# Loading four modulation chunks ahead of the tokens in the prologue of a fused two-block transformer kernel

## What is computed

```
silu_c, silu_cc = silu(c), silu(c_ctx)
mod_lat = silu_c  @ ada_w[0] + ada_b[0]      # 6 x 1024: sh1, sc1, ga1, sh2, sc2, ga2
mod_ctx = silu_cc @ ada_w[0] + ada_b[0]
u_lat = rms_norm(h_lat, g_mix[0]) * (1 + sc1) + sh1
u_ctx = rms_norm(h_ctx, g_mix[0]) * (1 + csc1) + csh1
q, k, v = split(u_lat @ na_wqkv[0]), and the same for u_ctx
```

## Time and profile before

| what | value |
|---|---|
| time, median of 3 runs | 2734.12 us |
| lowest and highest of them | 2729.07 and 2738.08 us |
| the profiled execution's own time | 2735.49 us |
| its span, first to last instruction | 2733.7 us |
| mean granted clock of TensorE | 0.992 |
| TensorE busy | 2619.9 us, 96% of the span |
| VectorE busy | 1549.0 us, 57% |
| ScalarE busy | 1072.7 us, 39% |
| GpSimd busy | 875.9 us, 32% |
| sixteen DMA engines | 26.3% of their span |

### The profile page before, as it was taken

The page is one execution under the profiler, slowest core; times in us unless marked ns, Lnnn a source line. Parts: engine busy times, 40 slices in busy tenths (PEclk is TensorE's granted clock), DMA queues, the critical chain, the costliest instruction groups (busy, mean ns, idle before and its releaser), DMA issues. The chain is left out here.

```text
span 2733.7 us, 38265 instructions
## 1 busy us (share of the span) xinstructions
PE 2619.9 (96%) x14748; PEld 2129.2 (78%) x14748; DVE 1549.0 (57%) x2903; ACT 1072.7 (39%) x1864; POOL 875.9 (32%) x651
## 2 busy tenths in 40 slices
PE   6899999999999999999899999999999999999997
PEld 4787786788888888766668888787778888788886
DVE  5434444687777778555664444544556445516555
ACT  4444544422222223565542322354553434542222
POOL 1211121243333333021124444333334333444443
PEclk9999999999999999999999999999999999999999
DMA  6323333223333332110012222322213221222221
GB/s 246 114 86 96 113 101 101 85 104 106 106 105 106 106 107 72 52 47 32 32 47 95 105 92 92 96 64 76 77 48 102 69 86 62 94 93 93 93 93 62
DMA packets 69652, 243.02 MB, mean 89 GB/s; under 512 B 11780, under 2 KB 29700, under 8 KB 49288
## 3 DMA queue, kind: packets, MB, share of 16 engines
q1 hardware_dynamic: 69512, 241.15, 26.3%
HBM read 239.02 MB, written 2.10 MB: 88 GB/s over the span
## 5 line engine op out<-in xcount | busy, mean ns | idle before, releaser
L248 POOL TENSOR_TENSOR w_lo<-w_raw,w_hi 128x512 fp32r<-128x512 f32 x612 | 820.8, 1373 | 1737.3 <-ACT w_hi L241 604.9
L287 PE MATMUL bank<-u_hi,w_hi 128*128 128x512 f32 (+1 forms) x1952 | 732.3, 375 | 10.8 <-DVE u_lo L548 5.0
L289 PE MATMUL bank<-u_hi,w_lo 128*128 128x512 f32 (+1 forms) x1952 | 719.6, 369 | 0.0
L288 PE MATMUL bank<-u_lo,w_hi 128*128 128x512 f32 (+1 forms) x1952 | 718.7, 368 | 0.0
L287 PEld LDWEIGHTS bank<-u_hi,w_hi 128*128 128x128 f32 x1952 | 368.6, 189 | 82.0 <-issue 10.7
L288 PEld LDWEIGHTS bank<-u_lo,w_hi 128*128 128x128 f32 x1952 | 368.8, 189 | 62.1 <-issue 2.5
L289 PEld LDWEIGHTS bank<-u_hi,w_lo 128*128 128x128 f32 x1952 | 368.4, 189 | 62.5
L1088 DVE SCALAR_TENSOR_TENSOR resid<-bank,mod,resid 128x512 f32<-128x512 f32 (+1 forms) x384 | 242.1, 658 | 141.2 <-PE bank L289 136.4
L287 PE MATMUL bank<-hid_hi,w_hi 128*128 128x512 f32 (+1 forms) x768 | 275.5, 359 | 0.0
L289 PE MATMUL bank<-hid_hi,w_lo 128*128 128x512 f32 (+1 forms) x768 | 273.0, 355 | 0.0
L288 PE MATMUL bank<-hid_lo,w_hi 128*128 128x512 f32 (+1 forms) x768 | 272.1, 354 | 0.0
(11 more groups left out here) (411 smaller groups left out, 3885.3 us busy)
## 6 DMA issues: line engine op xcount, KB each, us to landing
w_raw<-stream SPq DMA_DIRECT2D x150, 1024.0 KB, 4.9
w_raw<-stream SPq DMA_DIRECT2D x56, 512.0 KB, 4.5
ada_ring<-stream SPq DMA_DIRECT2D x48, 512.0 KB, 4.7
bias<-bias SPq DMA_DIRECT2D x192, 64.0 KB, 2.3
ada_more<-stream SPq DMA_DIRECT2D x6, 1024.0 KB, 12.4
resid<-h SPq DMA_DIRECT2D x2, 1536.0 KB, 9.2
w_raw<-stream SPq DMA_DIRECT2D x8, 256.0 KB, 3.9
out<-resid SPq DMA_DIRECT2D x8, 256.0 KB, 2.0
```

The costliest lines, as they stand in the source:

```text
L248: ins = eng.tensor_tensor(m.wl[:, s, w], m.raw[:, s, w], m.wh[:, s, w].bitcast(F32), ALU.subtract)
L287: pe.matmul(out, lh, rh, start=start, stop=False)
L288: pe.matmul(out, lh, rl, start=False, stop=False)
L289: return pe.matmul(out, ll, rh, start=False, stop=stop)
```

## The change

SyncE issues modulation chunks 0 to 3 first, then the lower tokens, the weight chunk and the upper tokens; chunks 4 to 7 stand behind them as before. TensorE and VectorE do rows, copies, columns and gains of pairs 0 and 1 ahead of the norm's adds and sum. The rows of chunks 4 and 5 stand behind the norm's sum, ahead of projections 0 and 1; columns 2 and the rows of chunks 6 and 7 stand between projections 1 and 2, columns 3 between projections 3 and 4. On VectorE the copy of row 4 stands ahead of round 0, that of row 5 ahead of round 1; pair 2's columns and the copies of rows 6 and 7 ahead of round 2, pair 3's columns ahead of round 3. On ScalarE the high part of the weights moves from behind the eighth square to behind the fourth. In `na_stage` SyncE waits for the low part of the first weight chunk before it loads the next one into the same slot, which the wait for chunk 4's row implied before.

```diff
@@ Norm.act
             if k == KT // 2:
+                between()
                 act.wait_ge(second, 16)
             act.activation(self.sq[:, k % 2, :], m.h[:, k, 0:tok], ACT.Square).then_inc(*A.mark(f"n_sq{k}"))
-        between()
@@ prologue, vector
+                for p in range(2):
+                    copy(2 * p)
+                    copy(2 * p + 1)
+                    modulated(p)
                 norm.dve(dve)
...
+                def beside(p):
                     if p == 0:
+                        copy(4)
+                        own(dve, D)
                         dve.wait_ge(A.sem, A.at("n_rs"))
-                latent.dve(dve, 2, modulated)
+                    if p == 1:
+                        copy(5)
+                    if p == 2:
+                        modulated(2)
+                        copy(6)
+                        copy(7)
+                        own(dve, D)
+                    if p == 3:
+                        modulated(3)
+                        own(dve, D)
+                latent.dve(dve, 2, beside)
@@ prologue, tensor
-                rows(0)
-                rows(1)
-                norm.pe(pe)
+                for p in range(2):
+                    rows(2 * p)
+                    rows(2 * p + 1)
+                    columns(p)
                 pe.matmul(m.bank[:, 5, 0:2], cst(m, "ones"), m.misc[:, 2:4], start=True,
                           stop=True).then_inc(*E.mark("lamdot"))
-                columns(0)
+                norm.pe(pe)
+                rows(4)
+                rows(5)
                 pe.wait_ge(m.G.sem, m.G.at("w0_lo"))
-                for p in range(FIRST // 2):
-                    if 2 * p + 2 < FIRST:
-                        rows(2 * p + 2)
-                        rows(2 * p + 3)
-                    first_projection(2 * p)
-                    if 2 * p + 2 < FIRST:
-                        columns(p + 1)
-                    first_projection(2 * p + 1)
+                first_projection(0)
+                first_projection(1)
+                columns(2)
+                rows(6)
+                rows(7)
+                first_projection(2)
+                first_projection(3)
+                columns(3)
+                for k in range(4, KT):
+                    first_projection(k)
@@ na_stage, sync
                 load_bias(0, 2, bias_last_in)
+                sp.wait_ge(*m.first_low)
                 for n in range(2, 5):
                     load(fills[n])
```

More of the change, by code:

```diff
@@ L617, in prologue @@
                        only=0)
[L618 to L623, removed]
+        A.plan(["exp_c"] + Norm.act_steps[:KT // 2] + ["w0_hi"] + Norm.act_steps[KT // 2:] + ["exp_lam"])
+        pairs = [(f"row{2 * p}", f"row{2 * p + 1}", f"mod{p}", f"gsc{p}") for p in range(FIRST // 2)]
+        D.plan(["eps", "zero", "sig1", "sig2", "silu", "sel", *pairs[0], *pairs[1]] + Norm.dve_steps +
+               ["q1", "q2", "q3", *pairs[2], *pairs[3], "lam1", "lam2"])
+        E.plan(["ada0", "ada1", "columns0", "ada2", "ada3", "columns1", "lamdot", "n_sum", "ada4", "ada5", "columns2",
+                "ada6", "ada7", "columns3"])
         m.G.plan(["w0_lo"])
         m.ring_read = E.sem, E.at("ada4")
+        m.first_low = m.G.sem, m.G.at("w0_lo")
         for block in (m.block,):
@@ L631, in _, with chunk @@
                 sp.dma_start(m.cst[:, :], m.in_cst[:, 0:CST["swap"][1]]).then_inc(m.small_in, 16)
[L632 to L635, removed]
+                def chunk(n):
                     if n >= 4:
@@ L638, in _ @@
                         sp.wait_ge(landed[n % 4], 16 * (n // 4))
-                    sp.dma_start(slots[n % 4], m.stream[c]).then_inc(landed[n % 4], 16)
+                    sp.dma_start(slots[n % 4], m.stream[ORDER[n]]).then_inc(landed[n % 4], 16)
+                for n in range(4):
+                    chunk(n)
+                sp.dma_start(m.h[:, 0:KT // 2, :], m.in_h[:, 0:KT // 2, :]).then_inc(h_in, 16)
+                sp.dma_start(m.raw[:, 0, :], m.stream[N_ADA]).then_inc(m.first_in, 16)
+                sp.dma_start(m.h[:, KT // 2:KT, :], m.in_h[:, KT // 2:KT, :]).then_inc(rest_in, 16)
+                for n in range(4, FIRST):
+                    chunk(n)
             @block.scalar
@@ L681, in _, with copy, modulated @@
                                   ALU.add).then_inc(*D.mark("sel"))
+                def copy(n):
+                    dve.wait_ge(E.sem, E.at(f"ada{n}"))
+                    if n >= 2:
+                        dve.wait_ge(E.sem, E.at(f"columns{n // 2 - 1}"))
+                    dve.tensor_copy(part[:, n % 2, :], m.bank[:, 2 + n % 2, 0:2 * P]).then_inc(*D.mark(f"row{n}"))
+                def modulated(p):
+                    dve.wait_ge(E.sem, E.at(f"columns{p}"))
+                    mod_add(dve, m, pmod[:, 4 * p:4 * p + 4], p)
+                    mod_add(dve, m, pmod[:, 16 + 4 * p:20 + 4 * p], 4 + p).then_inc(*D.mark(f"mod{p}"))
+                    own(dve, D)
+                    mod_gain(dve, m, 4 + p).then_inc(*D.mark(f"gsc{p}"))
+                for p in range(2):
+                    copy(2 * p)
+                    copy(2 * p + 1)
+                    modulated(p)
                 norm.dve(dve)
```

## The result

The changed kernel takes **2737.0 us** (median of 13 runs, 2734.71 to 2743.15), the kernel before 2733.3 (13 runs, 2728.89 to 2738.08). Paired, the ratio is **1.0019, interval 1.0011 to 1.0027**: slower by 5.2 us, 3.0 to 7.4. That is no change by the 0.3% named ahead, and yet it can be told from zero. The forecast was 2736.6 and +2.5 us. (The two medians lie 3.7 us apart; the 5.2 is the paired ratio less 1, times 2733.)

A forecast was written before the change was run, and what follows sets the result against it. Bound: when the prologue hands on the first projection. First scaling 8.8 us later less 7.1 of gaps gives +1.7 (+1.2 to +4.6 by TensorE's clock); +2.5 chosen on the median 2734.12, so 2736.6 us, range 2729.5 to 2743.

The forecast's parts named there:

- the hand-over: Start of ScalarE's squares of the first projection, 54.11 before; forecast at 55 to 58.5 us.
- Landings: Prologue loads: lower tokens land at 19.2 instead of 9.28, behind 4 MiB more at 2.49 us per MiB.
- The adds: Norm on VectorE: one square of 0.84 and four adds of 1.05 left; sums ready at 30.6, before 19.05.
- From the sums to the first scaling: Sums at 30.6, then TensorE's sum, row 4 and its copy; first scaling at 35.4, 8.8 us later than before.
- The gaps: VectorE's waits for TensorE between rounds: 2.2 us instead of 9.33, a gain of 7.1; 2 to 5 as sign.
- The term with the clock in it: TensorE's clock falling early in the projections moves round 3 by 2.9 us, giving the upper end of +4.6.
- The sum: Whole change: +8.8 us at the start less 7.1 in gaps is +1.7; +2.5 chosen between +1.2 and +4.6.
- The shift is handed on: Later stages: later work waits on this stage alone, so the shift passes on whole; 54.11 becomes 55.8.
- +1.5 us either way: Later stages: their own slow-clock stretches may move, worth about 1.5 us of either sign.
- The small gain: Rival: clock rises during the sums and stays up, start 8.3 later, gaps 2.2; −1.5 us, 2732.6; chance 0.17.
- The low clock through all rounds: Rival: TensorE stays slow through the rounds and bounds them; +13.7 us, 2748; chance 0.07.
- The third: Rival: copies 4 and 5 or columns late, gaps near 5; +4.5 us, 2738.6; counted in the forecast's 0.72.

The follow-up runs named there:

- The first two experiments: First: low part behind the adds, against the changed kernel, ratio 1.0006. Second: high part between squares, against the kernel before, ratio 1.0004.
- low part behind the adds: Changed kernel plus one wait: GpSimd starts the first weight chunk's low part only behind the norm's last add; ratio 1.0006 to the kernel before.
- busy ahead of the sums: Changed kernel with low part behind the adds, plus 14 useless TensorE matmuls ahead of the norm's sum; ratio 1.0020 to the kernel before.
- the same, busy twice: Busy ahead of the sums, plus four more useless matmuls behind chunk 5's row, in TensorE's idle stretch; ratio 1.0021 to the kernel before.
- high part between squares: Kernel before, loads in its order, with only the weights' high part moved from behind the eighth square to behind the fourth; ratio 1.0004.
- copy behind the round: Changed kernel with low part behind the adds, VectorE's copy of row 4 moved behind the first round; ratio 1.0009 to the kernel before.
- two chunks ahead: Changed kernel with low part behind the adds, two modulation chunks instead of four ahead of the tokens; ratio 1.0011 to the kernel before.
- copies in the round, cold: Copies in the round, busy, without its 12 useless matmuls; ratio 0.9994 to the kernel before.
- sum first, busy start: Before, busy start, with the norm's sum ahead of modulation chunk 1's row on TensorE; ratio 0.9988 to the kernel before, 2728.38 us.
- before, busy start: Kernel before plus 12 useless TensorE matmuls ahead of its first row; ratio 0.9985, 2728.53 us.
- copies in the round, busy: Sum first, busy start, with the next pair's copies inside each round and columns ahead of both projections; ratio 0.9988 to the kernel before, 2728.5 us.

## Why the prediction was right or wrong

The whole time came out within 0.4 us of the forecast, and this flatters it; in part it is luck. The shift is 5.2 us where +2.5 was chosen, the median of before came out 0.8 lower than the one that the forecast started from, and the hand-over (60.35) lies outside the 55 to 58.5 that the prediction named. Its own steps:

**Landings: right.** The tokens came at 18.77 (19.2 was forecast), and 2 MiB less ahead of them gave back 5.05 us. The second pair's modulation ended at 17.65, ahead of the first add at 20.38, so modulating early was hidden as said.

**The adds: the step that failed.** "One square of 0.84 and four adds at 6.27 / 6 = 1.05 are left: the sums are ready at 30.6." They were ready at 33.12. The price of an add was taken from the earlier trace rows, where GpSimd stood still, and the paragraph put GpSimd's 4.95 us into the very same window without asking what the two do to each other. Four adds took 7.21 instead of 4.2, +3.0. The tokens' 0.4 took some of that back. The low part took 7.08 instead of 4.95. The first two experiments show the pair as the cause, from both sides: taken apart in the changed kernel the adds are at 4.14 again, and put together in the kernel before they take 7.23. The Trainium skill, "SBUF — State Buffer", in "Who interferes with whom", says that a VectorE instruction with two SBUF inputs contends with a GpSimd instruction that reads SBUF, as both kinds do here. By that rule the trace agrees.

**From the sums to the first scaling: 0.6 short.** 4.8 was forecast, 5.38 was measured. The sum took 2.93, not the 2.36 of the earlier trace rows: before, two chunks ran straight ahead of it, here it follows 15.76 us of idle. 2.93 is its time wholly at the slow rate (it recurs in five of the experiments; the two executions of before had 2.36 and 1.81, partly at the full rate), 1.56 at the fast one. The forecast had kept the old duration as its slow end.

**The gaps: 3.64 for 2.2 to 5.** The term with the clock in it was right in kind. The first gap was 0.25 and the third 0.37 (0.45 and 0.46 forecast). The second, 3.02, has both first projections at the low clock. With four useless matmuls in the idle stretch it is 1.35, where the prediction had 1.3 for a clock that stays up. So the low clock costs about 1.7 us in the changed kernel, inside the 0 to 2.9 given.

**The sum.** With the low part behind the adds the prologue is the one that I had reckoned with: first scaling 34.83 (35.4), gaps 3.45 (2.2 to 5.1), hand-over +2.40 (+2.5). Of the 3.84 us that the changed kernel loses beyond that at the hand-over, 3.67 lie in the start of the first scaling: 3.06 in the adds beside the low part, 0.31 in tokens that landed later in its execution, and 0.30 in the two chunks behind the sum, which ran at the slow rate for longer. The overlap is the 3.06. That the hand-over agrees so well with +2.5 is some luck too: the first scaling came 0.6 early, and the gaps were 0.4 over the 3.0 that +2.5 stands for.

**The shift is handed on: open in part.** The prediction said that later work waits on this stage alone, and named a deviation of over 5 us as the sign against it. Over all kernels (shift of the hand-over in one profile, against ratio − 1 times 2733):

| kernel | hand-over, us | time, us (interval) |
|---|---|---|
| changed | +6.2 | +5.2 (3.0 to 7.4) |
| busy ahead of the sums | +4.0 | +5.5 (2.5 to 8.2) |
| low part behind the adds | +2.4 | +1.6 (−0.5 to 4.1) |
| the same, busy twice | +1.3 | +5.7 (3.3 to 7.9) |
| high part between squares | +0.7 | +1.1 (−1.4 to 3.3) |
| copy behind the round | +0.3 | +2.5 (0 to 5.2) |
| two chunks ahead | −0.1 | +3.0 (0.5 to 5.2) |
| copies in the round, cold | −3.5 | −1.6 (−4.1 to 0.8) |
| sum first, busy start | −4.6 | −3.3 (−5.7 to −1.1) |
| before, busy start | −5.2 | −4.1 (−6.6 to −1.6) |
| copies in the round, busy | −6.5 | −3.3 (−6.0 to −0.8) |

The order is kept on the whole, and a line through the points rises by 0.8 us per us, from +1.5 at a hand-over that doesn't move. But three hand-overs lie outside the interval of the time, by 0.5, 0.6 and 2.0 us, and all three kernels took longer than their hand-over says. One of them is the kernel with four matmuls in the idle stretch, 4.4 us too long. Its profile has the low clock for 6.8 us near 132 and for 10.2 near 463, where the first experiment had none and 3.4. By activation numbers it is 2.7 us ahead of the kernel with the matmuls ahead of the sums alone up to 135, and 0.6 behind that first place. The kernel with the matmuls ahead of the sums alone has the stretch of 10.2 us too. The places and costs of such stretches are shown; that a kernel's prologue decides how often they come is not shown, and one profile of each kernel can't show it. That stays open. The "+1.5 us either way" that the prediction allowed for them was too little: between two executions of one kernel they came to 5.5.

**The rivals.** The small gain needed a start 8.3 later and didn't get it. The low clock through all rounds didn't come: it held for 3.4 us. The third, that the move changes nothing for the rounds, had a fitting size (+4.5) for a wrong reason, since the gaps did shrink by 5.7.

## What to carry to other kernels

A duration is a price only together with what ran beside it: before putting two engines' work into one window, look whether the row that gives the price had the other engine idle. Work that is moved ahead of a load on the same queue costs its full transfer time there (here 2.5 us per MiB), and pays only if it removes more waiting than that; here four chunks put the tokens off by 9.5 us and the first scaling by 8.2, and by 11.9 with the overlap, to save some 5.8. And ask of a stretch of waiting how much of it is the engine's slow clock: that share may go for a few useless instructions, with nothing moved. It may also not: fourteen matmuls ahead of the sums only brought TensorE to a longer wait behind them, with the low clock after it.

## What the runs showed of the hardware

- VectorE's add of two SBUF operands (128x768) takes 0.96 us alone and 4.14 for four; beside GpSimd's subtraction on SBUF four take 7.21, and the four subtractions go from 4.95 to 7.08. Neither stands still for the whole of the other: four adds at 0.96 and four subtractions at 1.24 are 8.8 us end to end, and the window was 7.9 (25.22 to 33.12). Two scalings, which read two SBUF tensors as well, go from 2.10 to 3.11 or 3.23.
- Twelve useless matmuls during the first loads make the kernel 0.15% faster: the sum goes from 2.36 to 1.56, a chunk from 1.86 to 1.07, and the slow stretch of the rounds is gone.
- A faster TensorE can come to a longer wait, and a low clock with it, in single executions: idle for 4.01 instead of 2.50 us, and a stretch at 0.50 of 6.8 us instead of 3.4; idle for 1.81 instead of 0.65, and two chunks in 3.38 instead of 1.93.
- One kernel's executions differ by up to 5.5 us of span through slow-clock stretches far behind the prologue (near 137, 470 and 1318 us). So a change of 5 us can't be read from one pair of profiles: these gave +1.2 and +7.6.
